# The beginning of a two-block transformer kernel: first chunks loaded in quarters, x turned between their products, products with high parts first, a later place for the next chunk's products

## The chip, the cores and the metric

One Trainium2 (trn2) chip, one of its cores. The metric is device time in microseconds (us) from one launch, the median of a few runs; lower is better.

## What is computed

The reference runs two blocks over x of 256 tokens by 1024 in float32. The first has two layers; each is a gated feed-forward part (1024 to 2 x 2816 and back), a mixer (pooling, then differential attention) and a second feed-forward part. Shift, scale and gate of every norm come from a conditioning row c. The second block mixes by block attention and a recurrent memory, and has one feed-forward part. At the beginning stand:

```python
c_act = jax.nn.silu(c)
for i in range(DEPTH):
    mod = (c_act @ mod_w[i] + mod_b[i])[:, None, :]
    sh0, sc0, g0, sh1, sc1, g1, sh2, sc2, g2 = jnp.split(mod, N_MOD, axis=-1)
    h = modulate(rms_norm(x, norm_g[i, 0]), sh0, sc0)
    x = x + 0.5 * g0 * swiglu(h, ffn_w_gu[i, 0], ffn_w_down[i, 0])
```

So the first feed-forward product needs the shift sh0 and the scale sc0, which are the first 2048 columns of silu(c) @ mod_w.

## The kernel before

All weights and activations are float32. A product of the feed-forward parts is made of three: both operands are split into a high part (rounded to the type that TensorE takes in one pass) and a low part (the rest), and high x high, low x high and high x low are added up in PSUM (`three`, lines 501 to 504).

**Weights.** They come as pieces of 1 MB, two transfers of 512 KB each (`load_gu` line 410, `load_down` line 417), asked for on SyncE's queue into a ring of three raw buffers. A raw buffer is free when the piece three before it has been split. ScalarE makes the high part (`make_hi`, line 1285), VectorE the low part (`make_lo`, line 1902). For the first feed-forward part pieces 0 to 3 are gate-and-up weights of the first two steps, 4 is the down weight, 5 and 6 gate-and-up of the third step, 7 its down weight; then 8 and 9 gate-and-up and 10 down, and so on. `split(k)` in ScalarE's and VectorE's programs is k times one of these.

**Modulation.** mod_w is used in chunks of 512 columns, 2 MB each, loaded by GpSimd's queue: `load_own_chunk` (line 2784) for the first four, `load_chunk` (line 2775) for the others, in halves of 1 MB. The chunks (0, 0) and (0, 1) are multiplied on TensorE as a row (`own_chunk`, line 620, float32 in two passes), whose row ScalarE copies (`keep_row`) and TensorE turns into a column (`turn_row`, line 629). All others are added up on VectorE, eight multiply-adds of 128 x 512 (`add_chunk`, lines 1940 and 1943), and TensorE turns the sum (`sum_chunk` line 602, `turn_chunk` line 611); `keep_chunk` and `keep_turned` store it. MOD_HEAD is chunk (0, 4), MOD_STEP the chunks (0, 5) and (0, 6), MOD_LOOP those from (0, 7) on. A chunk's load is allowed by the number of multiply-adds done (`acc_step`), and the load of (0, 5) also by the high part of piece 5 (`w_hi` 7).

**x.** It is normed and turned by TensorE as a product with a diagonal of the reciprocal norms (line 659), each token block of 128 in two halves of four tiles; `scaled_tiles` puts scale and shift on, for token block 0 on VectorE and for block 1 on ScalarE; `half_hi` and `x_lo` make its two parts (`nt_hi`, `nt_lo`). The first halves of both need chunks (0, 0) and (0, 2), the second halves (0, 1) and (0, 3). Ahead of `ffn(0, ...)` `keep_awake` issues 20 transposes that nobody reads.

**Order.** Nothing is scheduled by a planner: each engine's program is written out by hand and meets the others by semaphores. `first_head` (once in the program of TensorE, of ScalarE and of VectorE) holds the first two steps of the first feed-forward part. Banks T, A, M, B hold step 0 token 0, step 0 token 1, step 1 token 0 and step 1 token 1. Each is gated (`gated_half` on ScalarE, `product` on VectorE), turned (`turn_one`, line 593) and split (`hidden_hi`, `hidden_lo`) for the down product (`down_block`). `ffn_steps` then does `step(0)` and a loop of steps, in each of which `columns` multiplies two pieces for both tokens and `down_block` one; `turn_inner` is line 584. The two arguments of `step` that matter are `between` (a chunk turned between the two pieces) and `middle` (between the tokens of the down product).

## Time and profile before

| | |
|---|---|
| median of 3 runs | 1376.66 us (1376.52 to 1376.71) |
| span of the profiled execution | 1376.3 us |
| TensorE (PE) busy | 1330.4 us, 97% |
| VectorE (DVE) busy | 947.7 us, 69% |
| ScalarE (ACT) busy | 643.6 us, 47% |
| mean granted TensorE clock | 0.992 |
| read from HBM | 302.91 MB, 221 GB/s over the span |

In the profile's rows, PE is TensorE's matmuls and PEld its weight loads, DVE is VectorE, ACT ScalarE, POOL GpSimd, SPq the queue of SyncE. A timeline's row gives the start, the length, the engine, the line, the tiles and the count, and in brackets how long the engine sat idle before it and what ended that. The length of a row of pipelined matmuls is longer than their distance from start to start. GpSimd's loads run in queue q0, SyncE's in q1; both use the same 16 transfer engines.

### The profile page before, as it was taken

To read this page: it belongs to the slowest core of one execution; us is meant where nothing else is said; L and a number is where in the kernel's file an instruction comes from. 1 tells how busy PE (TensorE), PEld (TensorE's weight loads), DVE (VectorE), ACT (ScalarE), POOL (GpSimd) and SP (SyncE) were. 2 spreads that over 40 slices of the span, in tenths; PEclk is the share of its full clock that TensorE was granted. 3 is DMA by queue.
4 is the path that set the end of the run, shared out by engine and by line. 5 is a ranking of instruction groups with operands and counts; after the bars stand their busy time and mean duration, and the time that the engine had idled before them with its cause. 6 is when DMAs were issued, how large, how long until landed. Compare 5 with 4: busy or idle time off the path is not lost.

```text
span 1376.3 us, 17805 instructions
## 1 busy us (share of the span) xinstructions
PE 1330.4 (97%) x6271; PEld 1083.9 (79%) x6271; DVE 947.7 (69%) x1125; ACT 643.6 (47%) x847; POOL 152.8 (11%) x215
## 2 busy tenths in 40 slices
PE   5999999999999999999998899999999999999997
PEld 3678888888888888888787688888887777888885
DVE  4788888789887788887577475465796656554442
ACT  3434334543333743335566543334655663643341
POOL 2100001200010100000331100010136000000000
PEclk9999999999999999999999999999999999999999
DMA  9999887499885798874633395564445434365540
GB/s 338 327 345 332 304 308 251 155 334 318 309 308 202 246 316 303 306 250 141 210 123 121 103 327 171 193 191 170 153 166 191 166 129 151 114 229 189 191 150 31
DMA packets 179926, 304.82 MB, mean 221 GB/s; under 512 B 8524, under 2 KB 122596, under 8 KB 179608
## 3 DMA queue, kind: packets, MB, share of 16 engines
q1 hardware_dynamic: 159288, 224.63, 47.9%
...
HBM read 302.91 MB, written 1.05 MB: 221 GB/s over the span
## 4 chain that ended last, share of the span: by engine, by line
PE 46%; ACT 3%; DVE 2%; issue 1%; POOL 0%; POOLq 0%; ACTq 0%; DVEq 0%
PE ps L502 14%; PE ps L504 14%; PE ps L503 14%; ACT whi L1285 1%; PE ps L931 1%; PE ps L951 1%; PE ps L584 1%; PE ps L657 0%; DVE wlo L1902 0%; DVE xres L2190 0%; DVE xn L2187 0%; ACT ps L1358 0%; ACT xn L1397 0%; PE ps L1063 0%; PE ps L940 0%
## 5 line engine op out<-in xcount | busy, mean ns | idle before, releaser
L1902 DVE TENSOR_TENSOR wlo<-raw,whi 128x2048 fp32r<-128x2048 f32 x212 | 482.4, 2298 | 95.8 <-ACT whi L1285 93.6
L502 PE MATMUL ps<-whi,nthi 128*128 128x512 f32 (+1 forms) x1264 | 507.0, 401 | 4.5 <-DVE ntlo L2226 1.7
L504 PE MATMUL ps<-whi,ntlo 128*128 128x512 f32 (+1 forms) x1264 | 493.8, 391 | 0.0
L503 PE MATMUL ps<-wlo,nthi 128*128 128x512 f32 (+1 forms) x1264 | 493.0, 390 | 0.0
L1285 ACT ACTIVATE whi<-raw 128x2048 fp32r<-128x2048 f32 x212 | 397.1, 1908 | 71.8 <-DMA raw<-in_ffn_w_gu 30.7
L502 PEld LDWEIGHTS ps<-whi,nthi 128*128 128x128 f32 x1264 | 239.3, 189 | 53.8 <-issue 5.8
L504 PEld LDWEIGHTS ps<-whi,ntlo 128*128 128x128 f32 x1264 | 238.6, 189 | 51.4
L503 PEld LDWEIGHTS ps<-wlo,nthi 128*128 128x128 f32 x1264 | 239.6, 190 | 45.4
L1943 DVE SCALAR_TENSOR_TENSOR arena<-arena,cact 128x512 f32<-128x512 f32 x238 | 178.7, 751 | 10.4 <-DMA arena<-in_mod_w 2.8
L502 PE MATMUL ps<-whi,hthi 128*128 128x512 f32 x440 | 172.7, 393 | 1.5 <-DVE htlo L1993 1.2
L504 PE MATMUL ps<-whi,htlo 128*128 128x512 f32 x440 | 171.6, 390 | 0.0
L503 PE MATMUL ps<-wlo,hthi 128*128 128x512 f32 x440 | 171.3, 389 | 0.0
L1319 ACT ACTIVATE arena<-ps 128x256 f32<-128x256 f32 x110 | 41.7, 381 | 225.1 <-PE ps L504 224.8
L1328 ACT ACTIVATE hthi<-ps 128x512 fp32r<-128x512 f32 x40 | 24.0, 599 | 195.7 <-PE ps L584 195.7
L502 PEld LDWEIGHTS ps<-whi,hthi 128*128 128x128 f32 x440 | 82.6, 188 | 18.9 <-issue 1.6
L504 PEld LDWEIGHTS ps<-whi,htlo 128*128 128x128 f32 x440 | 82.6, 188 | 17.3
L503 PEld LDWEIGHTS ps<-wlo,hthi 128*128 128x128 f32 x440 | 82.7, 188 | 16.7
L2775 POOL DMA_DIRECT2D arena<-in_mod_w x64 | 48.4, 757 | 415.5 <-DVE arena L1943 364.9
L1987 DVE TENSOR_TENSOR htlo<-ps,hthi 128x512 fp32r<-128x512 f32 x40 | 27.6, 690 | 94.8 <-ACT hthi L1328 94.8
L1974 DVE TENSOR_TENSOR arena<-arena,ps 128x256 f32<-128x256 f32 x110 | 43.6, 415 | 58.1 <-ACT arena L1319 57.4
L2811 POOL TENSOR_SCALAR ss<-ss 128x1 f32<-128x1 f32 x18 | 11.2, 625 | 514.5 <-ACT ps L1358 514.4
L1358 ACT ACTIVATE ps<-xres 128x1024 f32<-128x1024 f32 x18 | 18.5, 1027 | 63.7 <-DVE xres L2190 37.3
...
## 6 DMA issues: line engine op xcount, KB each, us to landing
...
```

The lines of the kernel that those rows point to most:

```text
L502: pe.matmul(o, hi, wh, start=start, stop=False)
L503: pe.matmul(o, hi, wl, start=False, stop=False)
L504: return pe.matmul(o, lo, wh, start=False, stop=stop)
L1285: nc.scalar.activation(whi[:, s * PIECE:(s + 1) * PIECE], raw[:, r * PIECE:(r + 1) * PIECE], ACT.Copy).then_inc(w_hi, 1)
L1319: nc.scalar.activation(sil[:, j, :], o[:, 0:FFW], ACT.Silu).then_inc(silu_done, 1)
L1328: nc.scalar.activation(hthi[:, par * BLK:(par + 1) * BLK], o, ACT.Copy).then_inc(ht_hi, 1)
L1358: nc.scalar.activation(junk, x[:, t, :], ACT.Square, accum_out=ss[:, t:t + 1]).then_inc(sq_done, 1)
L1902: v.tensor_tensor(wlo[:, s * PIECE:(s + 1) * PIECE], raw[:, r * PIECE:(r + 1) * PIECE], hi, ALU.subtract).then_inc(w_lo, 1)
L1943: e = v.scalar_tensor_tensor(acc, src[k // 4][:, k % 4, :], cact[:, k:k + 1], acc, ALU.mult, ALU.add)
L1974: v.tensor_tensor(sil[:, j, :], sil[:, j, :], ps[:, b, FFW:2 * FFW], ALU.mult).then_inc(drained[b], 1)
L1987: v.tensor_tensor(htlo[:, at], ps[:, T, :], hthi[:, at].bitcast(F32), ALU.subtract)\
L2775: pool.dma_start(mbuf[mod_place(c.first)][h], src[:, 4 * h:4 * h + 4, bass.ds(chunk * MCH, MCH)])\
```

## The change

- GpSimd loads each half of the first four chunks as two quarters of 512 KB, with a semaphore each. Chunk (0, 0) goes ahead of (0, 2) in each pair. SyncE's weight loads wait for the same number of megabytes as before.
- TensorE's own products are made by halves (`own_half`), with the parameters' transposes and the turning of token block 0 between the halves of chunk (0, 0), and the two halves of block 1 before and after the row and the sums (`turn_first`). `keep_awake` of 20 is gone at this place.
- `both_tokens` takes piece 0 and piece 2 for both token blocks at once, four products with high parts first and the weights' low part as late as possible.
- The row of chunk (0, 1) is turned between halves of bank b. The order of turning and gating is T, A, M, B instead of T, M, A, B.
- On VectorE the multiply-adds of chunk (0, 4) stand behind piece 5 and behind `hidden_lo(1, 1, T)`, and pieces 7 and 8 stand together ahead of `keep_turned`; TensorE turns this chunk in `step(0)` between the pieces and not ahead of it.

```diff
--- before.py
+++ after.py
         mod_landed = [[sem(f"mod_landed{b}{h}") for h in range(2)] for b in range(2)]
-        first_landed = [[sem(f"first_landed{i}{h}") for h in range(2)] for i in range(4)]
+        first_landed = [[sem(f"first_landed{i}{q}") for q in range(4)] for i in range(4)]
...
-                    load_gu(gu, 0, 0, [(first_landed[2][1], 16)])
+                    load_gu(gu, 0, 0, [(first_landed[0][3], 16)])
                     load_gu(gu, 1, 0)
-                    load_gu(gu, 0, 4, [(first_landed[3][0], 16)])
+                    load_gu(gu, 0, 4, [(first_landed[3][1], 16)])
...
-            def own_chunk(i, lap):
-
-                o = bank(M)
-                for k in range(KT):
-                    if k % 4 == 0:
-                        pe.wait_ge(first_landed[i][k // 4], 16 * lap)
+            def own_half(i, o, h):
+
+                for k in range(4 * h, 4 * h + 4):
+                    if k % 2 == 0:
+                        pe.wait_ge(first_landed[i][k // 2], 16)
                     mm = pe.matmul(o[0:1, :], cact[:, k:k + 1], mfirst[i][k // 4][:, k % 4, :],
                                    start=(k == 0), stop=(k == KT - 1))
-                    if k == 3:
-                        mm.then_inc(first_used, 1)
-                mm.then_inc(filled[M], 1)
+                mm.then_inc(filled[M] if h else first_used, 1)
...
+            def turn_first(t, h):
+
+                if h == 0:
+                    pe.wait_ge(rdiag_ready, n.next("join").at + 1)
+                for q in range(4):
+                    o, c = ps[:, 2 * t + h, q * P:(q + 1) * P], slice((4 * h + q) * P, (4 * h + q + 1) * P)
+                    mm = pe.matmul(o, x[:, t, c], rdiag[:, t * P:(t + 1) * P], start=True, stop=True)
+                mm.then_inc(xt_done, 1)
...
+                def both_tokens(h, o0, o1):
+
+                    p = n.next("piece").first
+                    wh, wl = (w[:, p * PIECE:(p + 1) * PIECE].rearrange("p (k n) -> p k n", k=4) for w in (whi, wlo))
+                    pe.wait_ge(w_hi, p + 2)
+                    pe.wait_ge(nt_hi, 2 * h + 1)
+                    one(o0, h, nth, 0, wh, opens=(h == 0))
+                    pe.wait_ge(nt_lo, 2 * h + 1)
+                    one(o0, h, ntl, 0, wh)
+                    pe.wait_ge(nt_hi, 2 * h + 2)
+                    one(o1, h, nth, 1, wh, opens=(h == 0))
+                    pe.wait_ge(w_lo, p + 2)
+                    mm = one(o0, h, nth, 0, wl, closes=(h == 1))
+                    if h:
+                        mm.then_inc(filled[T], 1)
+                    pe.wait_ge(nt_lo, 2 * h + 2)
+                    one(o1, h, ntl, 1, wh)
+                    one(o1, h, nth, 1, wl, closes=(h == 1)).then_inc(w_used, 1)
+                def half(o, t, h, w, ks=range(4)):
+                    for k in ks:
...
-                w0 = views()
-                t0 = bank(T)
-                pe.wait_ge(nt_lo, 1)
-                half(t0, 0, 0, w0)
-                a = bank(A)
-                pe.wait_ge(nt_lo, 2)
-                half(a, 1, 0, w0).then_inc(w_used, 1)
-                own_chunk(1, 1)
+                t0, a = bank(T), bank(A)
+                both_tokens(0, t0, a)
+                o = bank(M)
+                own_half(1, o, 0)
+                own_half(1, o, 1)
                 w1 = views()
                 b = bank(B)
-                half(b, 1, 0, w1)
+                half(b, 1, 0, w1, (0, 1))
                 turn_row(gate[0:1, :])
+                half(b, 1, 0, w1, (2, 3))
                 sum_chunk()
                 m = bank(M)
                 half(m, 0, 0, w1).then_inc(w_used, 1)
-                w0 = views()
-                pe.wait_ge(nt_lo, 3)
-                half(t0, 0, 1, w0).then_inc(filled[T], 1)
+                both_tokens(1, t0, a)
                 w1 = views()
                 half(m, 0, 1, w1).then_inc(filled[M], 1)
                 turn_one(0, T, T)
-                pe.wait_ge(nt_lo, 4)
-                half(a, 1, 1, w0).then_inc(w_used, 1)
-                turn_one(1, M, M)
+                turn_one(1, A, A)
                 half(b, 1, 1, w1).then_inc(w_used, 1)
-                turn_one(0, A, A)
+                turn_one(0, M, M)
                 d0 = down_piece()
                 pe.wait_ge(drained[T], n.seen(T))
                 down_block(d0, 0, 0, True, False)
...
-                step(0, middle=turn_chunk if len(MOD_STEP[f]) == 2 else None,
+                step(0, turn_chunk if f == 0 else None, middle=turn_chunk if len(MOD_STEP[f]) == 2 else None,
...
                 if f == 0:
                     first_head()
-                    turn_chunk()
                 else:
...
             pe.wait_ge(cact_ready, 1)
-            own_chunk(0, 1)
+            own = bank(M)
+            own_half(0, own, 0)
             pe.wait_ge(prm_landed, 16 * 9)
...
             pe.transpose(o[:, 256:328], brow[1][:, :], ident[0:72, 0:72]).then_inc(filled[A], 1)
+            turn_first(0, 0)
+            turn_first(0, 1)
+            own_half(0, own, 1)
+            turn_first(1, 0)
             pe.wait_ge(consts_set, 3)
             turn_row(gate[0:1, :])
-            turn_join((0,))
             sum_chunk()
-            turn_join((1,))
-            keep_awake(T, 20)
+            turn_first(1, 1)
             ffn(0, mod_cols(0, 2))
...
 
                 split(1)
+                half_hi(0, 0)
                 act.wait_ge(xt_done, 3)
                 scaled_tiles(0, 1)
-                half_hi(0, 0)
                 half_hi(1, 0)
-                split(2)
+                split(1)
                 keep_row(gate[0:1, 0:BLK])
                 n.next(M)
                 split(1)
@@ -1496,12 +1517,13 @@
                 split(1)
                 gated_half(0, full(T))
                 split(1)
-                gated_half(1, full(M))
+                gated_half(1, full_at(A, 2))
                 hidden_hi(0, 0, T)
-                gated_half(0, full_at(A, 2))
+                gated_half(0, full(M))
+                hidden_hi(0, 1, A)
+                gated_half(1, full_at(B, 3))
+                split(1)
                 hidden_hi(1, 0, M)
-                gated_half(1, full_at(B, 3))
-                hidden_hi(0, 1, A)
                 split(1)
                 hidden_hi(1, 1, T)
                 split(4)
...
 
                 dve.wait_ge(drained[M], n.seen(M))
                 scaled_tiles(0, 1)
-                split(1)
                 x_lo(0, (0,))
+                split(1)
                 x_lo(1, (0,))
                 split(1)
                 add_chunk(3)
-                split(2)
                 keep_own_chunk(chunk_at(*MOD_FIRST[1]))
                 keep_chunk(chunk_at(*MOD_FIRST[3]))
                 dve.wait_ge(drained[M], n.seen(M))
                 scaled_tiles(4, 2)
                 x_lo(0, (1,))
+                split(1)
                 x_lo(1, (1,))
                 split(1)
                 pass_by(T)
                 product(0, T)
-
+                n.next(A)
+                product(1, A)
+                hidden_lo(0, 0, T)
+                split(1)
+                pass_by(M)
+                product(0, M)
+                hidden_lo(0, 1, A)
+                split(1)
                 c = add_chunk(halves=(0,))
-                pass_by(M)
-                product(1, M)
-                hidden_lo(0, 0, T)
-                split(1)
-                n.next(A)
-                product(0, A)
-                hidden_lo(1, 0, M)
-                add_chunk(halves=(1,), of=c)
                 n.next(B)
                 product(1, B)
-                hidden_lo(0, 1, A)
+                hidden_lo(1, 0, M)
                 split(1)
                 hidden_lo(1, 1, T)
-                split(1)
+                add_chunk(halves=(1,), of=c)
+                split(2)
                 keep_turned(chunk_at(*MOD_HEAD[0]))
 
                 c = add_chunk(halves=(0,))
-                split(1)
                 add_chunk(halves=(1,), of=c)
...
                 for h in halves:
                     if behind:
                         pool.wait_ge(*behind[h])
-                    pool.dma_start(mfirst[i][h], src[:, 4 * h:4 * h + 4, chunk * MCH:(chunk + 1) * MCH])\
-                        .then_inc(first_landed[i][h], 16)
+                    for q in (2 * h, 2 * h + 1):
+                        k = 2 * (q % 2)
+                        pool.dma_start(mfirst[i][h][:, k:k + 2, :], src[:, 2 * q:2 * q + 2, chunk * MCH:(chunk + 1) * MCH])\
+                            .then_inc(first_landed[i][q], 16)
...
             for h in range(2):
-                for j in (2, 0):
+                for j in (0, 2):
                     load_own_chunk(*MOD_FIRST[j], j, halves=(h,))
```

TensorE, the beginning of its program. Before:

```order
L620 MATMUL ps<-arena,cact 1x512 x8
L1253 MATMUL ps<-ident,arena 128x120
L1254 MATMUL ps<-ident,arena 128x72
L1255 MATMUL ps<-ident,arena 128x72
L629 MATMUL ps<-ones,gate 128x1 x4
L659 MATMUL ps<-rdiag,xres 128x128 x8
L602 MATMUL ps<-ones,arena 128x1 x4
L659 MATMUL ps<-rdiag,xres 128x128 x8
L666 MATMUL ps<-ident 128x128 x20
```

and now, with line 619 for the own products, 658 for x turned, 626 for the row and 724 for the products of `both_tokens`:

```order
L619 MATMUL ps<-arena,cact 1x512 x4
L1272 MATMUL ps<-ident,arena 128x120
L1273 MATMUL ps<-ident,arena 128x72
L1274 MATMUL ps<-ident,arena 128x72
L658 MATMUL ps<-rdiag,xres 128x128 x8
L619 MATMUL ps<-arena,cact 1x512 x4
L658 MATMUL ps<-rdiag,xres 128x128 x4
L626 MATMUL ps<-ones,gate 128x1 x4
L602 MATMUL ps<-ones,arena 128x1 x4
L658 MATMUL ps<-rdiag,xres 128x128 x4
L724 MATMUL ps<-whi,nthi 128x512 x4
L724 MATMUL ps<-whi,ntlo 128x512 x4
```

The own products of chunk (0, 0) are in two halves with x between them, the 20 transposes of line 666 are gone, and the products with `whi` stand ahead of those with `wlo`.

VectorE, from the low part of piece 5 on. Before (`arena<-arena,cact` is the adding up of a chunk, `wlo` a low part, `arena<-arena,ps` a gated half, `small<-ps` the keeping of a turned chunk), from the first multiply-adds of chunk (0, 4) to the last `htlo` of `first_head`:

```order
L1940 TENSOR_SCALAR arena<-arena,cact 128x512
L1943 SCALAR_TENSOR_TENSOR arena<-arena,cact 128x512 x3
L1974 TENSOR_TENSOR arena<-arena,ps 128x256
L2042 TENSOR_TENSOR htlo<-ps,hthi 128x2x128
L1902 TENSOR_TENSOR wlo<-raw,whi 128x2048
L1974 TENSOR_TENSOR arena<-arena,ps 128x256
L2042 TENSOR_TENSOR htlo<-ps,hthi 128x2x128
L1943 SCALAR_TENSOR_TENSOR arena<-arena,cact 128x512 x4
L1974 TENSOR_TENSOR arena<-arena,ps 128x256
L2042 TENSOR_TENSOR htlo<-ps,hthi 128x2x128
L1902 TENSOR_TENSOR wlo<-raw,whi 128x2048
L2042 TENSOR_TENSOR htlo<-ps,hthi 128x2x128
```

and behind them the low part of piece 7 and what follows it:

```order
L1902 TENSOR_TENSOR wlo<-raw,whi 128x2048
L1957 TENSOR_REDUCE small<-ps 128x4
L1959 TENSOR_TENSOR modc<-small,modb 128x4
L1940 TENSOR_SCALAR arena<-arena,cact 128x512
L1943 SCALAR_TENSOR_TENSOR arena<-arena,cact 128x512 x3
L1902 TENSOR_TENSOR wlo<-raw,whi 128x2048
L1943 SCALAR_TENSOR_TENSOR arena<-arena,cact 128x512 x4
L1902 TENSOR_TENSOR wlo<-raw,whi 128x2048
```

and now, from piece 5 on:

```order
L1924 TENSOR_TENSOR wlo<-raw,whi 128x2048
L1962 TENSOR_SCALAR arena<-arena,cact 128x512
L1965 SCALAR_TENSOR_TENSOR arena<-arena,cact 128x512 x3
L1996 TENSOR_TENSOR arena<-arena,ps 128x256
L2064 TENSOR_TENSOR htlo<-ps,hthi 128x2x128
L1924 TENSOR_TENSOR wlo<-raw,whi 128x2048
L2064 TENSOR_TENSOR htlo<-ps,hthi 128x2x128
L1965 SCALAR_TENSOR_TENSOR arena<-arena,cact 128x512 x4
L1924 TENSOR_TENSOR wlo<-raw,whi 128x2048 x2
L1979 TENSOR_REDUCE small<-ps 128x4
L1981 TENSOR_TENSOR modc<-small,modb 128x4
L1962 TENSOR_SCALAR arena<-arena,cact 128x512
```

Of chunk (0, 4) four multiply-adds stood ahead of piece 5's low part and stand behind it now; the other four moved behind the last `htlo`. The eight of chunk (0, 5) stood around piece 8 and stand behind it.

## Rows read from the trace of the kernel before

**Rows 1.** The page: busy time and share by engine; a costly group of ScalarE.
```profile
PE 1330.4 (97%) x6271; PEld 1083.9 (79%) x6271; DVE 947.7 (69%) x1125; ACT 643.6 (47%) x847; POOL 152.8 (11%) x215
...
L1319 ACT ACTIVATE arena<-ps 128x256 f32<-128x256 f32 x110 | 41.7, 381 | 225.1 <-PE ps L504 224.8
```

**Rows 2.** Waits of TensorE, 55 to 250 us: total, times, longest.
```profile
PE ps L611 <- DVE arena L1943: 2.3, 1, 2.3
```

**Rows 3.** TensorE's timeline at the gate; last row: a window (busy times, clock, DMA).
```profile
94.66 0.39 PE L503 MATMUL ps<-wlo,nthi 128*128 128x512 f32 x1
94.89 0.39 PE L504 MATMUL ps<-whi,ntlo 128*128 128x512 f32 x1
...
97.56 0.91 PE L611 MATMUL ps<-ident,arena 128*128 128x128 f32 x4 [2.28 <-DVE arena L1943]
...
98.00:101.00 3.00, 3.00 (x10) 2.41 (x9) 3.00 (x2) 1.28 (x1) 0.75 (x1) 0.50 0.99 363
```

**Rows 4.** VectorE's timeline from piece 8's low part to the gate.
```profile
79.88 2.29 DVE L1902 TENSOR_TENSOR wlo<-raw,whi 128x2048 fp32r<-128x2048 f32 x1 [2.46 <-ACT whi L1285]
...
85.11 2.28 DVE L1902 TENSOR_TENSOR wlo<-raw,whi 128x2048 fp32r<-128x2048 f32 x1
...
87.97 0.68 DVE L1957 TENSOR_REDUCE small<-ps 128x4 f32<-128x512 f32 x1
...
88.77 0.48 DVE L1940 TENSOR_SCALAR arena<-arena,cact 128x512 f32<-128x512 f32 x1
...
91.53 2.28 DVE L1902 TENSOR_TENSOR wlo<-raw,whi 128x2048 fp32r<-128x2048 f32 x1
...
...
97.35 4.49 DVE L1902 TENSOR_TENSOR wlo<-raw,whi 128x2048 fp32r<-128x2048 f32 x2
```

**Rows 5.** ScalarE's timeline: piece 8's high part.
```profile
77.93 1.92 ACT L1285 ACTIVATE whi<-raw 128x2048 fp32r<-128x2048 f32 x1 [6.39 <-DMA raw<-in_ffn_w_gu]
```

**Rows 6.** Timelines of GpSimd and of SyncE's queue: what they asked for.
```profile
59.98 2.23 POOL L2775 DMA_DIRECT2D arena<-in_mod_w  x3 [12.53 <-ACT whi L1285]
67.93 0.75 POOL L2775 DMA_DIRECT2D arena<-in_mod_w  x1 [5.72 <-DVE arena L1943]
...
64.19 0.99 SPq L410 DMA_DIRECT2D raw<-in_ffn_w_gu  x2
```

**Rows 7.** Queues, 64 to 68 us: packets, MB, share (q0 GpSimd's, q1 SyncE's).
```profile
q0 software_dynamic: 415, 1.57, 102.2%
q1 hardware_dynamic: 1, 0.00, 0.1%
```

**Rows 8.** Beginning: timelines, a window's clock, SyncE's queue from 14 to 17.
```profile
15.67 3.11 DVE L1943 SCALAR_TENSOR_TENSOR arena<-arena,cact 128x512 f32<-128x512 f32 x4 [2.76 <-DMA arena<-in_mod_w]
...
27.00 1.36 DVE L2035 TENSOR_SCALAR xn<-ps,scol,modc 128x128 f32<-128x128 f32 x4
...
28.99 1.16 ACT L1473 ACTIVATE nthi<-xn 128x512 fp32r<-128x512 f32 x2
...
18.41 3.59 PE L620 MATMUL ps<-arena,cact 128*1 128x512 f32 x8 [0.41 <-DMA arena<-in_mod_w]
...
26.43 2.03 PE L659 MATMUL ps<-rdiag,xres 128*128 128x128 f32 x16
...
31.31 0.47 PE L502 MATMUL ps<-whi,nthi 128*128 128x512 f32 x1 [0.67 <-DVE ntlo L2226]
...
36.96 7.03 PE L620 MATMUL ps<-arena,cact 128*1 128x512 f32 x16
...
48.96 1.02 PE L602 MATMUL ps<-ones,arena 128*128 128x1 f32 x8 [1.05 <-DVE modc L1950]
...
65.96 0.38 PE L593 MATMUL ps<-ident,arena 128*128 128x128 f32 x2
...
50.25:53.25 3.00, 3.00 (x7) 2.42 (x8) 2.16 (x7) 2.72 (x7) 0.00 (x0) 0.50 1.01 380
...
q1 hardware_dynamic: 1, 0.00, 0.0%
```

23 lines of the change are left out of this document (10 added, 13 removed).

## The prediction

> **What bounds the kernel now.** First the page: TensorE is busy for 97% of the span [rows 1]. A saving at the beginning is worth what it moves the point from which TensorE runs without a gap, and nothing more. Second, TensorE's waits from 55 to 250 us: one counts, 2.3 us at line 611 for VectorE [rows 2]. Third, TensorE's timeline there. Products follow each other every 0.23 us up to 94.89; then nothing until chunk (0, 6) is turned at 97.56, after 2.28 us of waiting, and from 98 to 101 the granted clock is 0.50, that is 1.2 of 2.4 GHz [rows 3]. Seven products take 3.0 us at that clock [rows 8], 1.4 us more than at the full one. I call 97.56 the gate: what TensorE wins ahead of it is lost unless VectorE opens it sooner.
>
> Fourth, VectorE's timeline back from the gate. From 79.88 to 97.35 it works without a gap, and 79.88 is the low part (line 1902) of weight piece 8 [rows 4]. Fifth, ScalarE had waited 6.4 us for that piece's transfer, to 77.93, and then made its high part in 1.9 us [rows 5]. Sixth, the issues: SyncE had asked for it at 64.19, so it took 13.7 us to be seen; GpSimd had asked for three halves of modulation chunks, 1 MB each, from 59.98 on and for a fourth at 67.93 [rows 6]. Seventh, the queues: between 64 and 68 us GpSimd's moved 415 packets and SyncE's one [rows 7]. So the gate is set by a weight transfer that stands behind chunk transfers, and then by VectorE's work.
>
> **The change, its start.** Chunk 0's second half becomes the third megabyte instead of the fourth; the third was used from 15.67, the fourth from 18.41 [rows 8]. But the parameters' transposes now stand ahead of it, and they wait for the small loads. SyncE's queue moved its last small packet after 14 [rows 8], so I put those at 15.0. Then 0.4 us of transposes, 2.0 of turning x, 3.6 for eight passes: 21.1, where before the passes ended at 22.0. Splitting the loads in two hides behind the full queue: GpSimd's issuing costs between what it did, 0.75 per megabyte, and twice that [rows 6], while the megabyte itself takes some 2.7 (15.67 to 18.41).
>
> From 22.0 to the first product at 31.31 took 9.3 us. Now there stand in a row: a quarter of x 1.0, the row 1.0, the sums 1.0, small waits 0.7, VectorE's tiles 1.4, ScalarE's high part 0.6 [rows 8], handing over 0.2. That is 5.9, for the other turnings, piece 0's low part and the 20 transposes that kept TensorE awake no longer stand ahead. First product at 27.0. The 24 products of both_tokens take 5.5 us and wait some 0.2 for the second token's high part: end at 32.7, before 36.9.
>
> From the second own chunk (36.96) to the end of b (65.96) was 29.0 us [rows 8]. The same 72 products and 16 passes stand there now. What goes is the wait of 1.05 ahead of line 602, since the row is turned between b's halves while VectorE has nothing else in hand; the 1.4 of slow clock behind it; and 0.4 of small waits. So 26.1, and b ends at 58.8, **7.2 us earlier**.
>
> **The change, VectorE's order.** ScalarE makes piece 5's high part right behind the gating of b, 0.4 + 1.9 us [rows 1, 5] and 0.3 of handing over. Its low part then starts at 61.4, against 61.67 before: the 7.2 us are gone, they were idle time of VectorE. And where half of chunk (0, 4) had been added up by then, all of it is still to do. From there to the gate VectorE has six low parts at 2.2, three whole chunks at 5.8 (2.8 for the half with the short first product, 3.0 for the other) and 3.9 of small work [rows 4, 8]: 34.5 us. If nothing is late, the gate opens at 95.9, 1.5 us sooner.
>
> Late next is piece 8. SyncE asks for it when piece 5's low part is done, at 63.7. GpSimd asks for two megabytes when piece 5's high part is done (61.4, before 59.98), for the third behind the half chunk (66.4), for the fourth at 72.6. It is the same four megabytes ahead of piece 8, starting 1.5 us later; piece 9, asked for when piece 6 is done, shares the queue a little sooner. I take piece 8 as seen at 77.9 + 1.5 = 79.4, and its low part from 81.4. The bounds: seen at 77.9 as before, or no wait at all, which is a low part at 74.8.
>
> Behind piece 8 stands more than before. Then it was 17.5 (79.88 to 97.35). Now keeping chunk (0, 4), 0.8, and the first half of chunk (0, 5), 2.8, stand there too: 21.0 [rows 4]. Gate: 81.4 + 21.0 = 102.4, **5.1 us later**. TensorE meets VectorE twice. It turns the last gated half at 66.7, and 12 + 24 + 24 + 12 products at 0.23, two turnings and 1.4 of slow clock later reaches chunk (0, 5), at 85.5; that opens at 90.2. From there 12 + 24 products, 1.2 of turnings and 1.4 of slow clock bring it to the gate at about 101.2, a wait of 1.2. At 2.28 the clock fell, ahead of 31.31 at 0.67 it did not [rows 3, 8]; I take it to stay up and give back 1.4: 5.1 - 1.4 = **+3.7 us**. Behind the gate TensorE has no wait of weight until 250 [rows 2], so the shift reaches the end. The profiled execution spans 1376.3, the median is 1376.66; added to the median that is 1380.4.
>
> The Trainium skill (DMA: Bandwidth & Descriptors, Queues, rings and completion order) says that each transfer engine goes round its queues packet by packet. By that piece 8 would take turns with the chunks and be no later than VectorE wants it, and the gate would come 1.5 us sooner. The trace has 415 packets to 1 against it.
>
> **The rivals.**
> Rival 1, piece 8 isn't late: the queues share once both have work ready, or piece 8 slips in ahead of the third megabyte, which is asked for 2.7 us behind it. For it: this third megabyte used to be asked for ahead of piece 8. Against: four microseconds in which SyncE's queue had an order and moved one packet [rows 7]. Then VectorE's work decides: gate at 95.9, TensorE there by 95, no slow clock, -1.5 - 1.4 = -2.9: 1373.8. It decides if piece 8 is seen by 72.9; each microsecond later costs one.
>
> Rival 2, half of that: piece 8 is seen at 75 to 77, the gate opens at 98 to 100, less 1.4: -0.8 to +1.2, so 1375.9 to 1377.9.
>
> Rival 3, the beginning is slower than summed: without the awake transposes the clock falls while x is turned in pieces. For it: small work with a gap of 1.05 ended in a clock of 0.50 from 50.25 on [rows 8]. Seven products at that clock cost 1.4 us, piece 5 moves to 63, all behind it with it: +5.3, 1382.0.
>
> Rival 4, piece 5 is ready at 60 (small loads by 13, b's end by 57) and piece 8 isn't late: -4.4, 1372.3.
>
> **How the numbers follow.** The likeliest case gets 0.45, with a range of its own of +1.5 to +6, since its largest term is one landing; rival 1 0.22, rival 2 0.15, rival 3 0.13, rival 4 0.05. About 0.2%, 2.75 us, can be told from no change. Slower by more: 0.38 of the likeliest and rival 3, 0.51. Within: 0.07 of the likeliest, rival 2 and 0.10 of rival 1, 0.32. Faster: 0.17. The range begins inside rival 1, at 1374.2, and ends above rival 3, at 1383.0.
>
> **What would show it.** First product near 27 and b's end near 59: the beginning is summed rightly. Then VectorE's low part of piece 8: 81 in my case, 75 in rival 1. A gap of TensorE from 86 to 90, where before was none, the gate at 102 and a granted clock of 1.00 behind it would confirm the rest. Either way TensorE should wait some 4 us ahead of 66.7, since VectorE adds half a chunk before the last gated half. If the gate opens before 97, I am wrong, and the first place to look is piece 8's landing; if it opens past 104, the first to look is the clock before 59.

## The result and the profile after

The changed kernel took **1383.93 us** (median of 4 runs, 1382.28 to 1386.28), the kernel before 1376.59 on the same chip: ratio 1.0048, 95% interval 1.0034 to 1.0061. Slower by 7.3 us; forecast were 1380.4 and a range up to 1383.0. Measured twice more on other chips, the ratio was 1.0024 (1.0013 to 1.0036) and 1.0029 (1.0019 to 1.0040), which is 3.6 and 4.0 us on the medians.

The page of the changed kernel:

```profile
span 1381.5 us, 17776 instructions
...
PE 1332.7 (96%) x6251; PEld 1084.3 (78%) x6251; DVE 947.0 (69%) x1125; ACT 643.6 (47%) x847; POOL 157.1 (11%) x223
```

TensorE's waits from 55 to 250 us (total, times, longest):

```profile
PE ps L611 <- DVE arena L1965: 5.5, 2, 3.0
PE ps L593 <- DVE arena L1996: 4.5, 2, 3.9
```

Where [rows 2] had one wait of 2.3, there are four now, 10 us in all. TensorE's timeline, first piece 0 (line 724 is `both_tokens`), then the last gated half (line 593), then chunk (0, 5) and the gate (line 611):

```profile
26.40 2.05 PE L724 MATMUL ps<-whi,nthi 128*128 128x512 f32 x4 [1.61 <-ACT nthi L1494]
28.25 1.74 PE L724 MATMUL ps<-whi,ntlo 128*128 128x512 f32 x4
29.82 1.09 PE L724 MATMUL ps<-whi,nthi 128*128 128x512 f32 x4
...
67.88 0.69 PE L593 MATMUL ps<-ident,arena 128*128 128x128 f32 x2 [3.93 <-DVE arena L1996]
...
88.95 0.66 PE L611 MATMUL ps<-ident,arena 128*128 128x128 f32 x4 [2.50 <-DVE arena L1965]
...
101.27 1.08 PE L611 MATMUL ps<-ident,arena 128*128 128x128 f32 x4 [3.01 <-DVE arena L1965]
```

Windows (the third number from the end is the granted clock, 0.50 being 1.2 GHz and 1.00 2.4 GHz):

```profile
25.00:30.00 5.00, 3.60 (x9) 2.91 (x10) 4.09 (x5) 4.34 (x7) 2.81 (x4) 0.66 0.99 354
...
100.00:105.00 5.00, 3.73 (x12) 3.11 (x13) 4.96 (x4) 0.46 (x1) 0.75 (x1) 0.66 0.96 333
```

The first product comes at 26.40 instead of 31.31 [rows 8], but after a wait of 1.61, and its first eight products run at the low clock (2.05 and 1.74 for four of them, 1.09 from then on). The gate opens at 101.27 instead of 97.56 [rows 3]. Behind it the clock is low again, as before the change.

ScalarE's timeline, the high part of piece 8:

```profile
77.89 1.91 ACT L1306 ACTIVATE whi<-raw 128x2048 fp32r<-128x2048 f32 x1 [7.09 <-DMA raw<-in_ffn_w_gu]
```

VectorE's, its low part and the first work behind the gate:

```profile
79.83 2.29 DVE L1924 TENSOR_TENSOR wlo<-raw,whi 128x2048 fp32r<-128x2048 f32 x1 [3.92 <-ACT whi L1306]
...
101.06 2.28 DVE L1924 TENSOR_TENSOR wlo<-raw,whi 128x2048 fp32r<-128x2048 f32 x1
```

GpSimd's and SyncE's, what they asked for:

```profile
62.70 1.49 POOL L2796 DMA_DIRECT2D arena<-in_mod_w  x2 [14.13 <-ACT whi L1306]
67.79 0.75 POOL L2796 DMA_DIRECT2D arena<-in_mod_w  x1 [3.59 <-DVE arena L1965]
...
64.98 7.84 SPq L410 DMA_DIRECT2D raw<-in_ffn_w_gu  x4
```

The queues from 65 to 68 us (packets, MB, share):

```profile
q0 software_dynamic: 300, 1.17, 98.0%
q1 hardware_dynamic: 2, 0.00, 0.0%
```

Piece 8 is seen at 77.89, to 0.04 us when it was before [rows 5]; its low part starts at 79.83, and from there VectorE works for 21.2 us without a gap where it had 17.5 [rows 4]. These 3.7 us are the gate's 3.7 us. From 65 to 68 the queues look as in [rows 7].

**Where the 7.3 us lie.** I follow line 584, TensorE's turning in each step. TensorE's timelines have the first one behind the gate, after:

```profile
114.28 0.60 PE L584 MATMUL ps<-ident,arena 128*128 128x128 f32 x4
```

and before:

```profile
110.84 0.66 PE L584 MATMUL ps<-ident,arena 128*128 128x128 f32 x4
```

That is +3.4, which holds within 0.3 us up to 945 us. At the last one, 1346.8 against 1341.5, it is +5.3. Between 945 and 1230 us 3.2 came at a low clock at 995 us that the profiled execution of before did not have, and 1.1 went again at 1157, where before had a low clock and after had none. The spans differ by 5.2. The rest is bookkeeping between single executions and medians, and names no cause. In every execution of these comparisons, whose time and span are both known, the time is 1.6 to 1.7 above the span; by that the profiled execution of before, with its span of 1376.3, took 1378.0, 1.4 more than the median of 1376.59. That of after, 1383.19, lies 0.7 under its own. 5.2 + 1.4 + 0.7 is 7.3.

### The profile page after: what moved, and what is told of

The parts are those of the page before. It is cut to its first block, busy times and chain, and to the rows that moved or that the text cites. A ratio compares the mean times of both kernels' runs of the same rounds, so it can differ in the third digit from the quotient of the medians.

```text
span 1381.5 us, 17776 instructions
## 1 busy us (share of the span) xinstructions
PE 1332.7 (96%) x6251; PEld 1084.3 (78%) x6251; DVE 947.0 (69%) x1125; ACT 643.6 (47%) x847; POOL 157.1 (11%) x223
## 3 DMA queue, kind: packets, MB, share of 16 engines
HBM read 302.91 MB, written 1.05 MB: 220 GB/s over the span
## 4 chain that ended last, share of the span: by engine, by line
PE 46%; ACT 3%; DVE 2%; issue 1%; POOL 0%; POOLq 0%; ACTq 0%; DVEq 0%
PE ps L502 14%; PE ps L504 14%; PE ps L503 14%; ACT whi L1306 1%; PE ps L949 1%; PE ps L969 1%; PE ps L584 1%; PE ps L649 0%; DVE wlo L1924 0%; PE ps L1081 0%; DVE xres L2211 0%; DVE xn L2208 0%; ACT ps L1379 0%; ACT xn L1418 0%; PE ps L958 0%
## 5 line engine op out<-in xcount | busy, mean ns | idle before, releaser
L502 PE MATMUL ps<-whi,nthi 128*128 128x512 f32 (+1 forms) x1248 | 499.9, 401 | 4.1 <-DVE ntlo L2326 1.3
L504 PE MATMUL ps<-whi,ntlo 128*128 128x512 f32 (+1 forms) x1248 | 487.5, 391 | 0.0
L503 PE MATMUL ps<-wlo,nthi 128*128 128x512 f32 (+1 forms) x1248 | 486.6, 390 | 0.0
L502 PEld LDWEIGHTS ps<-whi,nthi 128*128 128x128 f32 x1248 | 236.0, 189 | 52.7 <-issue 6.2
L504 PEld LDWEIGHTS ps<-whi,ntlo 128*128 128x128 f32 x1248 | 235.4, 189 | 50.5
L503 PEld LDWEIGHTS ps<-wlo,nthi 128*128 128x128 f32 x1248 | 236.2, 189 | 44.9
L504 PEld LDWEIGHTS ps<-whi,htlo 128*128 128x128 f32 x440 | 82.9, 188 | 17.5
```

Of the source, the lines that this page charges most:

```text
L502: pe.matmul(o, hi, wh, start=start, stop=False)
L503: pe.matmul(o, hi, wl, start=False, stop=False)
L504: return pe.matmul(o, lo, wh, start=False, stop=stop)
```

## The experiments

Every kernel was timed against the kernel before on its own chip (four groups of four kernels, each group on another chip; before had medians of 1377.75, 1376.71, 1377.43 and 1377.42, e1 to e4 being the first group, e5 to e8 the second, and so on). The expectations say each time what their theories are. "The mark" is line 584 behind the gate: 110.84 before, 114.28 after. The times of e4_sems are told with it.

| run | piece 8 seen | gate (wait) | mark | median us | ratio, 95% |
|---|---|---|---|---|---|
| e1_order | 81.63 | 102.43 (2.15) | 115.43 | 1381.37 | 1.0028, 1.0017 to 1.0038 |
| e2_awake | 76.66 | 100.04 (1.49) | 111.75 | 1380.26 | 1.0014, 1.0004 to 1.0024 |
| e3_shift | 78.73 | 98.38 (2.54) | 111.39 | 1379.53 | 1.0010, 1.0000 to 1.0020 |
| e5_after | 77.54 | 100.93 (2.98) | 113.97 | 1380.33 | 1.0024, 1.0013 to 1.0036 |
| e6_p8first | 76.40 | 99.79 (2.91) | 116.18 | 1381.08 | 1.0026, 1.0015 to 1.0037 |
| e7_order_p8 | 77.01 | 96.75 (2.98) | 117.19 | 1383.82 | 1.0046, 1.0034 to 1.0058 |
| e8_all | 74.60 | 94.56 (2.97) | 113.77 | 1383.34 | 1.0046, 1.0033 to 1.0060 |
| e9_lo2 | 78.14 | 101.53 (3.01) | 114.55 | 1381.40 | 1.0033, 1.0021 to 1.0045 |
| e10_lo24 | 77.97 | 101.36 (2.97) | 112.81 | 1379.95 | 1.0019, 1.0010 to 1.0028 |
| e11_best | 75.40 | 96.50 (3.32) | 109.36 | 1376.40 | 0.9993, 0.9984 to 1.0001 |
| e12_late5 | 78.35 | 97.99 (2.70) | 111.00 | 1379.12 | 1.0010, 1.0001 to 1.0018 |
| e13_b_order | 77.22 | 100.62 (2.97) | 113.62 | 1378.67 | 1.0006, 0.9995 to 1.0016 |
| e14_after | 79.12 | 102.51 (2.98) | 115.52 | 1381.39 | 1.0029, 1.0019 to 1.0040 |
| e15_ask | 75.38 | 98.78 (0.32) | 110.73 | 1378.13 | 1.0002, 0.9993 to 1.0011 |
| e16_b_ask6 | 72.96 | 96.36 (0.96) | 108.24 | 1374.52 | 0.9985, 0.9975 to 0.9994 |

From "piece 8 seen" to the gate it is 23.4 us in all three executions of the changed kernel and in e2, e6, e9, e10, e13 and e15, and 19.6 to 19.7 in before, e3, e4 and e12, which have VectorE's old order. (e7 and e8, with the old order too, have 19.7 and 20.0; in e1 and e11 VectorE waits in between, and e16 is told below.) So in these kernels the gate follows piece 8 at a fixed distance, and the new order makes this distance 3.7 us longer. The three executions of the changed kernel also show how far one profile can be off: piece 8 is seen at 77.89, 77.54 and 79.12, and the mark lies at 114.28, 113.97 and 115.52.

### e1_order: the changed kernel with VectorE's old order

```diff
                 product(1, A)
+                c = add_chunk(halves=(0,))
...
-                c = add_chunk(halves=(0,))
...
-                split(2)
+                split(1)
                 keep_turned(chunk_at(*MOD_HEAD[0]))
                 c = add_chunk(halves=(0,))
+                split(1)
                 add_chunk(halves=(1,), of=c)
```

> The changed kernel with VectorE's order of chunk products as near as possible to the old one: the first half of chunk (0, 4) right behind product(1, A), in the idle 2.3 us there, and keep_turned with the first half of chunk (0, 5) between the low parts of pieces 7 and 8. Theory 1 (the gate at 101.3 is piece 8's landing plus what stands behind it on VectorE): piece 8's low part stays near 79.8 (landing near 78), but 3.6 us less stands behind it, so the gate opens at 97.3 to 98, TensorE's wait of 3.9 us ahead of the last gated half shrinks to about 1, and the time falls by 3 to 4 us against the changed kernel, to 1379.5 to 1381. Theory 2 (the cost sits in the quarter loads and in slow clock, not in the order on VectorE): the gate may move, the time stays within 1 us of 1383.9.

The gate did not come sooner. VectorE now frees the half of a chunk before GpSimd asks, so GpSimd asks for three megabytes at once at 63.35, ahead of SyncE's piece 8, which is seen 3.7 us later than in the changed kernel. Behind it VectorE does have less to do: 18.6 us from its low part (83.58) to the gate's release (102.22), with 1.1 of waiting in them, against 21.2. What the old order saves behind piece 8 it loses in piece 8's landing. And since this kernel is nearly the new beginning alone, the new beginning by itself also opens the gate late: 102.43 against 97.56.

### e2_awake: 20 transposes ahead of `both_tokens`

```diff
             turn_first(1, 1)
+            keep_awake(T, 20)
             ffn(0, mod_cols(0, 2))
```

> The changed kernel with the 20 transposes that keep TensorE awake put back ahead of both_tokens. Theory 1: the first eight products run at the full clock (8 in 1.9 us and not in 3.4), b ends 0.5 to 1 us sooner, but the gate is held by piece 8 and by VectorE and moves by less than 0.5 us; total within 1 us of the changed kernel. Theory 2 (the slow clock at the start is passed on): total 1 us or more below the changed kernel.

TensorE's timeline:

```profile
24.29 2.35 PE L665 MATMUL ps<-ident 128*128 128x128 f32 x20
26.39 1.17 PE L724 MATMUL ps<-whi,nthi 128*128 128x512 f32 x4
27.41 1.08 PE L724 MATMUL ps<-whi,ntlo 128*128 128x512 f32 x4
```

The transposes fit into the wait: the first product starts at 26.39, and the first two rows of four take 1.17 and 1.08 instead of 2.05 and 1.74. What follows is 1.5 us sooner up to 66 us, and 1.2 from piece 8 on (76.66). The clock stays up behind the gate, so the distance from gate to mark is 11.7 us instead of 13.0. Of the 1.5 us of the start's low clock, 1.2 are passed on to the gate. The mark is then 0.9 behind before.

### e3_shift and e4_sems: kernel before, a time shift, and spare semaphores

```diff
-            keep_awake(T, 18)
+            keep_awake(T, 46)
```
```diff
         first_used = sem("first_used")
+        spare = [sem(f"spare{i}") for i in range(8)]
```

> The kernel before with 28 more transposes at full clock (3.3 us) in the mixer of the first layer, where TensorE keeps awake anyway; nothing ahead of 230 us changes. It tests whether the shift alone makes the second block slower. Theory A (where TensorE's slow clock falls in the second block depends on when it gets there): a stretch of granted clock 0.50 appears near 990 to 1005 us or moves there, and the time grows by 4 to 6 us, not 3.3. Theory B (the 2.1 us that the changed kernel loses between 945 and 1226 us come from something the change did to the program): the time grows by 3.3 us or less, no new stretch of low clock.

> The kernel before with eight more semaphores that nobody uses; the change has eight more (quarters instead of halves). The changed kernel's runs are 1.7 us longer than their spans, the kernel before's 0.4. Theory A (resetting the semaphores lies outside the span): span unchanged at 1376.3, time 1377.5 to 1378. Theory B (the number of semaphores costs nothing): time 1376.6, within 0.3.

Semaphores cost nothing: median 1377.22, ratio 0.9996 (0.9987 to 1.0005), and time less span is 1.67. TensorE runs 0.6 us behind before's profile at the mark and 1.1 at 730 us, so part of the 3.3 us of transposes fitted into waits. The shift cost 1.8 on the median, with an interval that reaches down to no change; its profiled execution had a low clock at 990 us that before's did not, and none at 1155, where before's had one. So an execution can win or lose such a stretch, though nothing near it was edited.

### e5_after and e14_after: the changed kernel on two more chips

> The changed kernel itself, again, beside the others of this call. Theory 1 (two losses, one of them fixed: +3.3 us at the gate, where piece 8 lands 0 us sooner than before and 3.5 us more of VectorE's work stands behind it; and one that falls differently in each execution: TensorE's slow clock, 2 us on the median): median ratio to before 1.003 to 1.006, and its executions spread by 3 us or more, with the spans longest where the mean granted clock is lowest (0.987 against 0.991 at one part in a thousand for each us). Theory 2 (the +7.3 us were a property of the first chip): ratio at or below 1.003, some +3 us.

> The changed kernel a third time, beside the others of this call. Theory 1: 3 to 4 us over before on the median, with single executions up to 8 us over where the mean granted clock is 0.987 or less. Theory 2 (the first chip's four executions, all 5.7 to 9.7 us over, are the rule): 6 us or more.

+3.6 and +4.0 on the medians. The first (ratio 1.0024) is what Theory 2 of e5_after expected, that some +3 us are the change and the rest was the first chip's own; the second is what Theory 1 of e14_after expected. That the first chip's four executions all lay higher stays unexplained; their mean clocks were 0.987 to 0.990, those of e5_after mostly 0.991.

### e6_p8first, e7_order_p8, e8_all: GpSimd waits for piece 8

```diff
             load_chunk(*MOD_STEP[0][0])
+            pool.wait_ge(w_hi, 10)
             load_chunk(*MOD_STEP[0][1])
```

e7_order_p8 adds the diff of e1_order, e8_all also that of e2_awake.

> The changed kernel; GpSimd asks for chunk (0, 6) only when the high part of piece 8 is made, so 2 MB of chunk (0, 5) are all that GpSimd asks for between piece 5 and piece 8. Theory 1 (piece 8 stands behind whatever GpSimd has asked for, and VectorE's work behind it sets the gate): from 62.7 four megabytes, 1 of piece 7, 2 of the chunk and 1 of piece 8, at some 0.38 MB/us: piece 8 is seen at 73 to 74, its low part starts at 75.9, when VectorE has nothing else (before this edit 79.83), the first gated chunk opens at 85 and TensorE, there at 86.5, does not wait; the gate at line 611 opens at 97.4 (was 101.27), and the kernel is 3 to 4 us faster than the changed kernel beside it. Theory 2 (the rate of the transfers as a whole binds, and piece 8's wait only moves to the chunk held back): piece 8 is seen earlier but chunk (0, 6) later, VectorE waits for the chunk ahead of the gate instead, gate at 100 to 102, time within 1 us of the changed kernel's.

> As the run before with GpSimd's wait for piece 8, and with VectorE's order of before (half of chunk (0, 4) added behind the first product, the rest and its keeping behind piece 7, half of chunk (0, 5) ahead of piece 8). With the old order alone piece 8 was seen at 81.6, and the gate did not open sooner. Theory 1: piece 8 is seen at 74 to 75, the work behind it is 17.5 us instead of 21, so the gate opens at 94 to 95 for VectorE; TensorE is there at 95 to 96 and does not wait, the clock stays up from 95 to 105. The start of the later blocks is 2.5 to 3.5 us sooner than in the kernel before; time 2 to 3 us under before. Theory 2: gate as in the run before, at 97 or later.

> As the run before, and 20 transposes ahead of both_tokens that keep TensorE's clock up. With those alone the first product came at the same time and all up to the gate was 1.2 us sooner. Theory 1: another 1 us on the run before, 3 to 4 us under the kernel before, if the gate then waits for neither; else the same as the run before. Theory 2: no difference from the run before.

The gate did open sooner, at 96.75 and 94.56, and the time was lost behind it. TensorE's timeline of e7_order_p8:

```profile
96.75 1.11 PE L611 MATMUL ps<-ident,arena 128*128 128x128 f32 x4 [2.98 <-DVE arena L1965]
...
117.19 1.11 PE L584 MATMUL ps<-ident,arena 128*128 128x128 f32 x4 [7.27 <-DVE arena L1996]
```

VectorE's timeline of it:

```profile
102.88 2.29 DVE L1924 TENSOR_TENSOR wlo<-raw,whi 128x2048 fp32r<-128x2048 f32 x1 [6.25 <-ACT whi L1306]
```

The held-back chunks leave as three megabytes at 79.22 and meet the weights of the next step, so VectorE waits 6.25 us for a high part and TensorE 7.27 for VectorE. In e6_p8first piece 8 gained only 1.1 to 1.5 us (against e5_after on the same chip, and against the first measurement), and VectorE waited 3.42 for a high part at 105.77, TensorE 3.21 for VectorE ahead of the mark. All three expectations of a gain fell; Theory 2 of e6_p8first (the wait only moves) comes nearest, though what waits is the weights and not the chunk. In these three kernels, what opened the gate by putting a transfer off was paid for behind the gate.

### e9_lo2, e10_lo24, e12_late5: is it the idle stretch of the transfers?

In the changed kernel the transfer engines stand at 0.30 from 45 to 50 us, since piece 2's low part comes 7 us later and piece 5 is asked for at 51.12 instead of 44.17.

```diff
                 keep_own_chunk(chunk_at(*MOD_FIRST[1]))
+                split(1)
                 keep_chunk(chunk_at(*MOD_FIRST[3]))
...
                 x_lo(0, (1,))
-                split(1)
```
```diff
                 product(1, A)
+                split(1)
                 hidden_lo(0, 0, T)
-                split(1)
```
```diff
-                    load_gu(gu, 2, 0)
+                    load_gu(gu, 2, 0, [(w_lo, 5)])
```

The first is e9_lo2, the first two together e10_lo24, the third, in the kernel before, e12_late5.

> The changed kernel with piece 2's low part made between the sums of the two own chunks (VectorE waits there 4.06 and 2.21 us in the changed kernel) and not behind them. Theory 3 (transfers bind: the changed order leaves piece 2's buffer in use until 51.0 instead of 44.1, so piece 5 is asked for 7 us later and the transfer engines stand at 0.30 between 45 and 50 us; 36 MB instead of 37 MB are in by 110 us, and at 0.35 MB/us that is the 3.3 us of shift): piece 5 is asked for at 45.6, the share of 45 to 50 us is over 0.8, more megabytes are in at 100 and 110, piece 8 is seen 1 to 3 us sooner, the gate opens at 99 to 100 and the block behind begins some 2 us sooner than in the changed kernel (114.3). Theory 1 (the queue was empty again at 60 to 62, so an idle stretch before that costs nothing; what GpSimd asks for from 62.7 on decides piece 8): transfers fill up earlier, piece 8 is seen within 0.5 us of 77.9, gate within 0.5 us of 101.3.

> As the run before, and piece 4's low part made ahead of the first hidden low part, where VectorE waits 2.28 us. Piece 7 is then asked for at 57.6 instead of 60.37, so the dip of the transfers at 60 to 62 us is gone too. Theory 3: another 1 to 2 us: piece 8 seen at 74 to 75.5, its low part at 76 to 77.5, gate at 97 to 99; kernel 3 us faster than the changed kernel. Theory 1: piece 7 leaves the queue ahead of the chunks, which takes 1 MB or 2.7 us from before piece 8 as well: piece 8 at 75 to 76 here, but not in the run before. The two theories differ in the run before, and agree here.

> The kernel before, with piece 5 asked for only when piece 3's low part is made (48.7) instead of piece 2's (44.1), and nothing else: the idle stretch of the transfers alone, without the change. Theory 3: some 1.2 MB fewer are in at 60 and stay missing at 80 and 100, piece 8 is seen 2 to 3 us later than 77.93, the gate opens 2 to 3 us later than 97.56, time 2 to 3 us over before. Theory 1: the transfers had a stretch at 0.69 from 57 to 60 in which this is made good; piece 8 and the gate within 0.5 us of before, time the same.

Theory 3 falls. With piece 5 asked for at 45.94 the gate stayed at 101.53; with it asked for at 48.72 in the kernel before, the gate moved by 0.4 and the mark by 0.2. In e12_late5 the transfers ran at 1.10 from 55 to 60 us, where before's had 0.83: the queue made it good, since before it was not full there (0.69 from 57 to 60). Its median is 1.7 over before's all the same, with an interval that nearly reaches no change. Of its profile's shift, 0.2 at 944 us, 1.2 at 1228, most comes at 1003, and it isn't the clock, which is 1.00 there in both executions: TensorE waits 0.70 for VectorE ahead of line 1073, where before's did not wait. Why VectorE was late there is open. In e10_lo24 piece 7 was asked for at 58.81 and not at 60.37. All of that execution ran a little later (piece 5's low part at 63.57, in the changed kernel 62.45), and piece 8 was seen 11.9 us after its ask instead of 12.9: one us of the 2.7 that Theory 1 counted. The gate did not move; the mark came 1.5 us sooner because the clock stayed up behind the gate.

### e13_b_order: kernel before, with VectorE's part of the change alone

```diff
-                c = add_chunk(halves=(0,))
                 pass_by(M)
...
                 hidden_lo(1, 0, M)
-                add_chunk(halves=(1,), of=c)
+                c = add_chunk(halves=(0,))
...
                 hidden_lo(1, 1, T)
-                split(1)
+                add_chunk(halves=(1,), of=c)
+                split(2)
                 keep_turned(chunk_at(*MOD_HEAD[0]))
                 c = add_chunk(halves=(0,))
-                split(1)
                 add_chunk(halves=(1,), of=c)
```

TensorE turns chunk (0, 4) in `step(0)` as in the changed kernel.

> The kernel before, with VectorE's part of the change alone: chunk (0, 4) added up behind piece 5, pieces 7 and 8 together ahead of keeping it, chunk (0, 5) whole behind piece 8, and TensorE's turning of (0, 4) moved to match. The beginning is that of before. Theory 1 (the gate is piece 8's low part plus the work behind it): piece 8 is seen at 77.5 to 78.5 as in both kernels, since the third megabyte of GpSimd's is asked for some 3 us behind it but goes first; 21 us of work stand behind its low part instead of 17.5, so the gate at line 611 opens at 101, 3.5 us later than 97.56; 3 to 3.5 us over before. Theory 4 (the shift comes from the beginning's new order of banks and products, VectorE's order only sets where TensorE waits): gate at 97 to 99, time within 1 us of before.

TensorE's timeline has both waits of the changed kernel, 2.50 and 3.01 there, with the beginning of before:

```profile
88.29 0.66 PE L611 MATMUL ps<-ident,arena 128*128 128x128 f32 x4 [1.90 <-DVE arena L1942]
...
100.62 0.68 PE L611 MATMUL ps<-ident,arena 128*128 128x128 f32 x4 [2.97 <-DVE arena L1942]
```

The gate is 3.1 us later, the mark 2.8, and from piece 8's low part to the gate VectorE works for 21.2 us as in the changed kernel: VectorE's order alone brings a loss at the gate of this size. It isn't the only half of the change that does. With the new beginning and the old order the gate was later still (e1_order, 102.43), so the two parts don't add up; both also change what GpSimd has asked for ahead of piece 8. What the beginning adds here can't be told from one profile: the changed kernel's mark is 0.7 behind e13's in the first measurement and 1.9 on the same chip (e14_after). Only 1.3 us of the loss show in the median of e13_b_order (interval -0.7 to +2.2), less than the 3 to 3.5 I expected, while the whole change costs 4.0 on this chip. So how the time is shared between the two parts is not shown. Its profiled execution had 1.1 us left of the 2.8 at 829 us. The low clock at 755 us, which before's profiled execution had, was missing there, so for the rest of the kernel the profile it is compared with is as much in doubt as its own.

### e15_ask, e11_best, e16_b_ask6: ask for chunk (0, 5) earlier

```diff
-            pool.wait_ge(w_hi, 7)
+            pool.wait_ge(w_hi, 6)
             load_chunk(*MOD_STEP[0][0])
```

This line in the kernel before is all of e16_b_ask6. e15_ask is the changed kernel with it, the two low parts of e10_lo24, and piece 5's high part ahead of the last `gated_half` of `first_head`; e11_best adds e1_order's order of the chunks and e2_awake's transposes.

> The changed kernel with what is asked for earlier and nothing else: pieces 2 and 4 get their low parts early, piece 5 its high part ahead of the last gating, and chunk (0, 5) is asked for behind piece 4's high part. VectorE's order of the changed kernel for the chunks, no awake transposes. Theory 1: piece 8 is seen at 73 to 75.5 instead of 77.9, 21 us behind it open the gate at 97 to 98.5, some 3 us sooner than in the changed kernel and level with before; with the order of before this was 96.5. So of the 4 us that all parts together win, the asks give 3 and order and awake transposes 1.

> The changed kernel with all that the runs so far point to: the two low parts early, piece 5's high part ahead of the last gating of the head, chunk (0, 5) asked for behind piece 4's high part instead of piece 5's, VectorE's order of before for chunks (0, 4) and (0, 5), 20 transposes ahead of both_tokens. Theory 3: the transfers are full from 5 us on, over 1 MB more is in at 70 than in the changed kernel, piece 8 waits for nothing, TensorE waits less than 2 us in all between 60 and 130; the block behind begins at 107 to 109 (before 110.84), time 2 to 4 us under the kernel before. Theory 1: the gate opens at 94 too, but TensorE then meets the weights behind it, as in the two runs with GpSimd's wait, and is back at before's time.

> The kernel before, with chunk (0, 5) asked for behind piece 4's high part (54.9) instead of piece 5's (59.98), one number. Theory 1 (what GpSimd has asked for when SyncE asks for piece 8 decides when piece 8 lands): piece 8 is seen at 73 to 75 instead of 77.93, its low part starts at 75 to 77, the gate opens at 95, when TensorE gets there, and the clock stays up: 2 to 3.5 us under before. Against it: piece 7, asked for at 57.3, now stands behind the two megabytes; if it comes later than 66.7 the gain is smaller. No gain at all if the transfers' full rate to the gate is what binds.

GpSimd's timeline of e16_b_ask6:

```profile
55.14 1.49 POOL L2775 DMA_DIRECT2D arena<-in_mod_w  x2 [7.40 <-ACT whi L1285]
61.49 0.75 POOL L2775 DMA_DIRECT2D arena<-in_mod_w  x1 [4.87 <-DVE arena L1943]
```

ScalarE's, the high part of piece 8:

```profile
72.96 1.92 ACT L1285 ACTIVATE whi<-raw 128x2048 fp32r<-128x2048 f32 x1 [1.31 <-DMA raw<-in_ffn_w_gu]
```

VectorE's, behind piece 8's low part, which starts at 77.45 without a wait:

```profile
86.75 0.69 DVE L1957 TENSOR_REDUCE small<-ps 128x4 f32<-128x512 f32 x1 [1.12 <-PE ps L611]
```

TensorE's, the gate:

```profile
96.36 0.65 PE L611 MATMUL ps<-ident,arena 128*128 128x128 f32 x4 [0.96 <-DVE arena L1943]
```

Its queues from 65 to 68 us:

```profile
q0 software_dynamic: 247, 0.96, 84.2%
q1 hardware_dynamic: 80, 0.21, 18.0%
```

Piece 8 is asked for at 64.31, as before, and seen after 8.65 us instead of 13.7: the two megabytes went in a stretch in which the transfers had stood at 0.83 (55 to 60 us; 1.05 now). VectorE's low part of it starts 2.4 us sooner. The gate opens only 1.2 us sooner, since VectorE is now early enough to wait 1.12 for TensorE's turning of chunk (0, 5); before, TensorE had turned it first. TensorE waits 0.96 at the gate instead of 2.28 and keeps its clock; the mark is 2.6 us sooner. One number makes the kernel before **2.9 us faster on the medians** (2.1 by the ratio, interval 0.8 to 3.4), the only one of these kernels whose interval lies wholly under the kernel before. In the changed kernel the earlier asks bring the mark from 114.28 to 110.73, level with before, as expected; beside e14_after, on the same chip, piece 8 is seen 3.7 us sooner, the gate opens 3.7 sooner, and the median is 3.3 lower. This is the closest test of the gate's cause: only the asks and the places of three splits moved. The order and the transposes on top brought 109.36 and 1376.40, which can't be told from before. The gate of 94 to 95 that I expected for e11_best and e16_b_ask6 did not come (96.50, 96.36).

## Why the prediction was wrong

In short: the gate was late for the reason I gave and by nearly the amount, partly by luck; the sum's last step, that a shift at 110 us reaches the end unchanged, was wrong.

**The gate, right in its mechanism, with one term mis-sized.** Piece 8's landing sets it, and then VectorE's work behind it, as forecast. Forecast were 21.0 us of work, it was 21.2. Piece 8 was seen 1.5 us sooner than the 79.4 I took, at my lower bound of 77.9, and the low part followed at 79.83, 1.6 us before my 81.4. So VectorE was done at 101.06 and not at 102.4, and the gate moved by 3.7 us and not by 5.1. The mis-sized term is the landing, "it is the same four megabytes ahead of piece 8, starting 1.5 us later". GpSimd's asks started 2.7 us later (62.70 against 59.98), and SyncE's by 0.8 (64.98 against 64.19). But only three megabytes went ahead of piece 8. The fourth was asked for at 74.00, 6 us later than before: GpSimd's queue moved 3.1 MB from 64 to 76 us, then next to nothing until 78, where before it had moved 4.2 MB by 77. At the 2.7 us per megabyte of the prediction, one fewer makes good the later start, and that piece 8 was seen within 0.04 us of before is this coincidence.

**"I take it to stay up and give back 1.4", wrong.** Chunk (0, 5) was turned at 88.95 (forecast 90.2), and from there TensorE needed 9.3 us to the gate and not 11.0, since the low clock that I had put behind this chunk did not come. So it waited 3.01 us at the gate and not 1.2, and there the clock fell as before. The two errors, 1.4 at the gate and 1.4 of clock, cancel: forecast +3.7, measured +3.4 at the mark. This agreement is luck.

**The beginning.** The own products ended at 20.3 (forecast 21.1, the small loads coming by 14.5 and not 15.0), the first product came at 26.40 (27.0). Then rival 3, with 0.13, came true in its mechanism: without the awake transposes the clock fell, the first 24 products took 7.2 us instead of 5.6 in e2_awake, and b ended at 60.0, not at 58.8. I priced rival 3 at 1.6 us over the likeliest case; e2_awake puts it at 1.5 at the start and 1.2 at the gate. Its forecast of +5.3 in all did not come, since piece 8 landed sooner. The wait of 3.93 ahead of line 593 is the forecast "some 4 us".

**"Behind the gate TensorE has no wait of weight until 250 [rows 2], so the shift reaches the end", wrong.** This is the step that failed. It put all that can change behind the gate at nothing, in the sum and in the range. Of waits up to 250 us it is true, of the clock further on it is not: the two profiled executions are 3.4 us apart at the mark and 5.2 at the end, by low stretches of the clock at 995 us in one and at 1157 in the other. Low stretches at 755 to 785, 990 to 1000, 1155 and 1370 us come and go from one execution to the next.

"Added to the median that is 1380.4" hides a second part. I set a change worked out against one execution on a median of 1376.66, as if 0.4 us lay around the span of 1376.3. It is 1.65, so that execution took 1.3 us more than the median. Counted from its own time the forecast would have been 1381.7, still inside my range, so this alone doesn't explain the miss. The remaining 2.1 of the 7.3 us, which is where the two profiled executions lie against their medians, have no cause on record. On the other chips the loss was 3.6 and 4.0 us. My estimate, from the 2 us that came behind 945 us here, is that such a range should be wider by about 2 us on either side, whatever the change.

These stretches start behind waits that all executions share. TensorE's timeline of the changed kernel, first measurement:

```profile
759.64 1.68 PE L969 MATMUL ps<-arena 128*128 128x128 f32 x8 [1.54 <-ACT arena L1667]
```

a window of it:

```profile
760.00:765.00 5.00, 5.00 (x23) 4.43 (x22) 1.55 (x3) 1.45 (x6) 0.89 (x2) 0.66 0.60 186
```

The same kernel in e5_after:

```profile
759.17 1.16 PE L969 MATMUL ps<-arena 128*128 128x128 f32 x8 [1.54 <-ACT arena L1667]
```

and its window:

```profile
760.00:765.00 5.00, 4.39 (x27) 3.60 (x26) 1.46 (x4) 2.44 (x8) 0.89 (x2) 1.00 0.63 204
```

Same kernel, same wait of 1.54, low clock in one and full clock in the other; between 626 and 829 us the second gains 1.6 us on the first. The Trainium skill (TensorE: Matmul & The Clock Gate, What's actually happening) says that the gate judges TensorE by a clock that runs free of the kernel, so that where the speed changes differs from run to run. By that rule a shift of the whole program by some tenths of a us can win or lose such a stretch; the two executions here agree with it, and e3_shift, 1.1 us behind before at 730 us, had another set of stretches than before. That the phase is the cause is not shown.

**Rivals 1 and 2** (piece 8 not late) were wrong here. In the kernel before, with one ask earlier (e16_b_ask6), piece 8 is not late: seen at 72.96, at the bound of 72.9 that I named, the gate opened without a loss of clock, and the mark came 2.6 us sooner where rival 1 had 2.9. It is another kernel, so this bears out rival 1's mechanism and not its sum.

**The rule on packets.** In 65 to 68 us 300 packets of GpSimd's queue went against 2 of SyncE's, as in [rows 7]. The Trainium skill (DMA: Bandwidth & Descriptors, Queues, rings and completion order) has the engines take turns between queues packet by packet. I read that as piece 8 being in time, and took one window as evidence against the rule. Both go too far. Where both queues move, the trace agrees with the rule: 68 packets to 73 from 69 to 70 us in before, 72 to 74 and 76 to 74 in the two us from 73 on in after. But GpSimd's packets carry 4 KB here and piece 8's 1 KB, so those 72 to 74 packets are 0.29 MB to 0.08, and with equal turns piece 8 still gets a fifth of the bytes.

The silent stretch is the time from piece 8's ask to its first packets, 3 to 4 us in before, in after and in e16_b_ask6 too. That kernel has 247 packets to 80 from 65 to 68, but 49 of the 80 go in the first us, with 0.16 MB: by their size they are the rest of piece 7. What differs is what comes next. The queues from 66 to 70 us, the changed kernel and then e16_b_ask6:

```profile
q0 software_dynamic: 390, 1.53, 97.7%
q1 hardware_dynamic: 72, 0.07, 5.6%
...
q0 software_dynamic: 232, 0.87, 57.5%
q1 hardware_dynamic: 569, 0.59, 44.5%
```

Asked for 5 us earlier, most of GpSimd's first three megabytes were through by 68 us, and piece 8 had the engines nearly to itself. Why the first packets take 3 to 4 us is open.
